# The gain multiplication of a norm moved from VectorE to GpSimd, behind the residual additions

## What is computed

```python
def rms_norm(x, g):
    xf = x.astype(jnp.float32)
    y = xf * lax.rsqrt(jnp.mean(xf * xf, axis=-1, keepdims=True) + RMS_EPS)
    return (y * g.astype(jnp.float32)).astype(x.dtype)

    for layer in range(DEPTH):
        h = h + FFN_RES_SCALE * swiglu(rms_norm(h, ffn1_norm[layer]), ...)
        hn = rms_norm(h, mix_norm[layer])
        ...
        h = h + attention(hn) @ w_o
        h = h + FFN_RES_SCALE * swiglu(rms_norm(h, ffn2_norm[layer]), ...)
        if layer == N_A_LAYERS - 1:
            kv = (rms_norm(h, kv_norm) @ kv_w)
    return rms_norm(h, final_norm)
```

## Time and profile before

| | us |
|---|---|
| three runs | 1777.2, 1777.74, 1778.76 |
| median | 1777.74 |
| profiled execution, first to last instruction (span) | 1775.5 |
| TensorE busy | 1757.9 (99%) |
| VectorE busy | 1184.5 (67%) |
| ScalarE busy | 869.8 (49%) |
| GpSimd busy | 63.4 (4%) |

### The profile page before, as it was taken

How to read it: one execution, slowest core, us unless ns; L and a number is a source line. 1 busy time by engine, 2 the same in 40 slices (tenths; PEclk the granted TensorE clock), 3 DMA queues, 4 the chain that set the end, 5 groups by cost and what they waited for, 6 DMA issues and landing times.

```text
span 1775.5 us, 24760 instructions
## 1 busy us (share of the span) xinstructions
PE 1757.9 (99%) x9869; PEld 1512.3 (85%) x9871; DVE 1184.5 (67%) x1245; ACT 869.8 (49%) x1082; POOL 63.4 (4%) x102
## 2 busy tenths in 40 slices
PE   9999999999999999999999999999999999999998
PEld 7888888888888888888888888888888888788887
DVE  7676576557576575557666666666676666876665
ACT  7545464445555464446343566533354434553343
POOL 1000000000120000000000100000000000210000
PEclk9999999999999999999999999999999999999999
DMA  9526355555556355555655553556556555246652
GB/s 322 179 91 218 119 190 191 190 191 191 187 165 211 133 172 189 189 190 177 201 179 189 194 165 121 177 190 206 178 185 202 179 189 187 98 156 198 196 182 95
DMA packets 215394, 318.03 MB, mean 179 GB/s; under 512 B 5617, under 2 KB 175745, under 8 KB 215314
## 3 DMA queue, kind: packets, MB, share of 16 engines
q1 hardware_dynamic: 210514, 300.96, 50.8%
q0 software_dynamic: 4800, 15.94, 2.8%
HBM read 315.83 MB, written 1.05 MB: 178 GB/s over the span
## 4 chain that ended last, share of the span: by engine, by line
PE 92%; DVE 3%; ACT 3%; issue 1%; POOL 0%; DMA 0%; DVEq 0%; ACTq 0%
PE Y L2094 29%; PE C L1930 22%; PE C L1934 12%; PE C L2033 4%; PE C L1996 3%; PE Y L1907 3%; PE Y L1996 2%; PE C L1998 2%; PE Y L1983 1%; PE Y L1998 1%; ACT w_hi L692 1%; PE C L2052 1%; ACT arena L1010 1%; PE C L2171 1%; PE Y L2306 1%
## 5 line engine op out<-in xcount | busy, mean ns | idle before, releaser
L1232 DVE TENSOR_TENSOR w_lo<-raw,w_hi 128x2048 fp32r<-128x2048 f32 x276 | 631.8, 2290 | 284.6 <-ACT w_hi L692 284.4
L692 ACT ACTIVATE w_hi<-raw 128x2048 fp32r<-128x2048 f32 x282 | 538.5, 1910 | 258.0 <-PE Y L2094 161.4
L1930 PE MATMUL C<-at_hl,w_hi 128*128 128x512 f32 x1424 | 339.1, 390 | 0.0
L1930 PEld LDWEIGHTS C<-at_hl,w_hi 128*128 128x128 f32 x1424 | 264.9, 188 | 53.5
L2094 PE MATMUL Y<-w_hi,hid_h 128*128 128x512 f32 x696 | 216.9, 393 | 0.1
L2094 PE MATMUL Y<-w_lo,hid_h 128*128 128x512 f32 x696 | 215.0, 390 | 0.0
L2094 PE MATMUL Y<-w_hi,hid_l 128*128 128x512 f32 x696 | 214.6, 389 | 0.0
L1934 PEld LDWEIGHTS C<-at_hl,w_lo 128*128 128x128 f32 x1424 | 183.0, 191 | 7.2
L1934 PE MATMUL C<-at_hl,w_lo 128*128 128x256 f32 x1424 | 185.2, 283 | 0.0
L2094 PEld LDWEIGHTS Y<-w_lo,hid_h 128*128 128x128 f32 x696 | 130.7, 188 | 28.1
L2094 PEld LDWEIGHTS Y<-w_hi,hid_l 128*128 128x128 f32 x696 | 130.7, 188 | 27.9
(11 more groups left out here) (337 smaller groups left out, 2276.5 us busy)
## 6 DMA issues: line engine op xcount, KB each, us to landing
raw<-in_ffn_w_in SPq DMA_DIRECT2D x88, 1024.0 KB, 5.1
raw<-in_w_ff SPq DMA_DIRECT2D x64, 1024.0 KB, 5.5
raw<-in_ffn_w_out SPq DMA_DIRECT2D x44, 1024.0 KB, 5.1
raw<-in_w_mem_kv SPq DMA_DIRECT2D x16, 1024.0 KB, 5.8
raw<-in_w_qkv SPq DMA_DIRECT2D x12, 1024.0 KB, 5.3
raw<-in_sb_w_qkv SPq DMA_DIRECT2D x12, 1024.0 KB, 5.2
raw<-in_w_in_ab SPq DMA_DIRECT2D x8, 1024.0 KB, 9.7
raw<-in_w_mem_q SPq DMA_DIRECT2D x8, 1024.0 KB, 5.0
```

The costliest lines, as they stand in the source:

```text
L692: nc.scalar.activation(w_hi[:, n % RING, :], raw[:, n % RAW, :], ACT.Copy).then_inc(hi_split, 1)
L1232: V.tensor_tensor(w_lo[:, n % RING, :], raw[:, n % RAW, :], w_hi[:, n % RING, :].bitcast(f32), ALU.subtract).then_inc(lo_split, 1)
L1930: mm(tiles(C[:, 2 * pair + i, :], 2), wh[:, k, i * P:(i + 1) * P], hl[:, k, :, :], start=k == 0, stop=False)
```

## The change

GpSimd multiplies x by g into `xn`, in two halves per block, as soon as x of the block is ready, and VectorE then multiplies each half in place by r. ScalarE's squares go to a stretch of the arena named `unread`. The list `gained_norms` takes the norms that are `("norm", "ahead")` with an `add` step just before. The diff, whole but for its context:

```diff
@@ build
         relu = [front[:, i * 2 * S:(i + 1) * 2 * S] for i in range(3)]
+        unread = front[:, 0:D]
@@
+        x_gained = sem("x_gained")
@@ behind the counts
+        gained_norms = [at.norm for (s, at), last in zip(before[1:], net) if s == ("norm", "ahead") and last[0] == "add"]
+
+        def x_parts(at):
+
+            return 4 * gained_norms.index(at.norm)
@@ GpSimd, behind the load of the weight row
                         pool.dma_start(gain[:, i % 2, :], gain_rows[i].partition_broadcast(P)).then_inc(gains_in[i % 2], 16)
+                if at.norm in gained_norms and s == ("norm", "ahead"):
+                    pool.wait_ge(gains_in[at.norm % 2], 16 * ((at.norm + 1) // 2))
+                    for b in range(TB):
+                        pool.wait_ge(x_ready, at.x - 1 + b)
+                        for i in range(2):
+                            part = slice(i * 512, (i + 1) * 512)
+                            nc.gpsimd.tensor_tensor(xn[:, b, part], x[:, b, part], gain[:, at.norm % 2, part], ALU.mult).then_inc(x_gained, 1)
@@ ScalarE
-            def guess(src, b, at, shift=0):
+            def guess(src, b, at, shift=0, to=None):
                 j = 2 * at.rms + b
-                nc.scalar.activation(xn[:, b, :], src, ACT.Square, accum_out=stat[:, 0, j:j + 1]).then_inc(squared, 1)
+                nc.scalar.activation(xn[:, b, :] if to is None else to, src, ACT.Square, accum_out=stat[:, 0, j:j + 1]).then_inc(squared, 1)
@@
-            def x_guess(b, at, shift=0):
+            def x_guess(b, at, shift=0, to=None):
                 act.wait_ge(x_ready, at.x - 1 + b)
-                guess(x[:, b, :], b, at, shift)
+                guess(x[:, b, :], b, at, shift, to)
@@ ScalarE, add_ahead
-                x_guess(0, then)
+                x_guess(0, then, 0, unread)
                 hi(then.chunk - 1 + AHEAD)
                 norm_hi("at", then, C, [0])
-                x_guess(1, then)
+                x_guess(1, then, 0, unread)
@@ VectorE
+            def gained_scale(b, at):
+
+                rms(b, at, 0)
+                j = 2 * at.rms + b
+                for i in range(2):
+                    part = xn[:, b, i * 512:(i + 1) * 512]
+                    dve.wait_ge(x_gained, x_parts(at) + 2 * b + i + 1)
+                    V.tensor_scalar(part, part, stat[:, 6, j:j + 1], None, ALU.mult).then_inc(xn_ready, 1)
@@ VectorE, add_ahead
                 add(factor, at, [0])
-                norm_scale("at", then, [0], 0, 2)
+                gained_scale(0, then)
                 add(factor, at, [1])
                 norm_lo("at", then, C, [0])
                 if doubled:
                     lo_part(then.chunk - 1 + AHEAD, 0)
-                    norm_scale("at", then, [1], 0, 2)
+                    gained_scale(1, then)
@@
                 lo_part(then.chunk - 1 + AHEAD, 0)
-                norm_scale("at", then, [1], 0, 2)
+                gained_scale(1, then)
```

## The result

The changed kernel takes 1780.29 us (median of 21 runs, 1780.03 to 1782.34), the kernel before in the same comparison 1777.48 (21 runs). The ratio is 1.0015, with a 95% interval of 1.0010 to 1.0021: 2.8 us slower. I had forecast 1777.5, with a range up to 1780.0.

What follows compares the result with a forecast made beforehand. TensorE bounds the kernel, leaving 1.84 us idle in five passages; terms of -0.10, 0, -0.35, +0.10 and +0.10 sum to -0.25 us, so 1777.74 becomes 1777.5, range 1775.6 to 1780.0.

Steps and rivals of the forecast that it cites:

- What bounds the kernel, and which passages: TensorE busy 1757.9 of 1775.5 us; five passages with 1.84 us idle; two behind an attention can't gain in block 0.
- second half of `w_lo`: Behind block 1's scaling, passages behind an attention: some 0.4 us later with 0.3 us slack, 0.1 lost each.
- VectorE's scaling: Two instructions of 1.41 us become two TENSOR_SCALARs: 0.45 us for the first half, 0.80 for both.
- GpSimd's products: Four per passage, 128x512, 1.04 us each; block 0's in time for VectorE by only 0.1 us.
- (d): GpSimd's product much longer than L606's: decides from about 1.3 us; at twice 1.04, +9 us, 1786.5; chance 0.07.
- The engines exclude each other: VectorE's refining and GpSimd's products wait for each other's whole instruction; block 0's refining ends 0.15 us later.
- Block 1: Stick passage: scaling starts at about 1007.1 instead of 1006.50, just in time; 0.10 gained booked for stick, 0 for `kv_cols`.
- no slack left: Said of block 1 in the stick passage, with GpSimd's products at 1.04 us each.
- The sign that I had named for being wrong: TensorE's turns of block 1 (L2171) waiting over 0.3 us would show the forecast wrong.
- The sum at my own price: Five passages with products at 1.04 us: -0.10 - 0 - 0.35 + 0.10 + 0.10 = -0.25 us.
- The row for "same": Its load goes out at about 1311.3, behind the `kv_cols` products; VectorE stalls 1.0 us, hidden with 1.5 to spare.
- The base: 1777.74 us for the kernel before, the span standing 2.2 us under the median of the runs.

Runs made afterwards that it cites:

- e8: Changed kernel with GpSimd multiplying only the first 512 columns, VectorE scaling the second half as before; 1776.25 us, ratio 0.9994 to the kernel before.
- e2: Changed kernel with GpSimd's product taking one repeated number per row, weight row left out of the five norms; 1777.03 us, ratio 0.9997 to the kernel before.
- e1: Changed kernel with the refining using one tensor input, other factors as numbers per token; 1777.02 us, ratio 0.9998 to the kernel before.
- e7: Changed kernel with the load of the row for "same" moved ahead of the products into kv_cols; 1780.27 us, ratio 1.0013 to the kernel before.
- e11: Changed kernel with GpSimd multiplying each half of x by the other half, weight row left out; 1780.1 us in a single execution.
- e6: Kernel before, with GpSimd also computing x times x into unused memory in the same four pieces; 1780.69 us, ratio 1.0019.
- e9: The first-half-only GpSimd product plus the refining with one tensor input, on the changed kernel; 1776.81 us, ratio 0.9994 to the kernel before.
- e3: Changed kernel without GpSimd products, VectorE scaling x by r alone, weight row left out of the five norms; 1776.10 us, ratio 0.9993 to the kernel before.

## Why the prediction was wrong

- **What bounds the kernel, and which passages.** Right: TensorE, five passages, two of them without a wait for the scaling in block 0. Those two still lost 0.35 each, by block 1's second half of `w_lo`; I had that place and sign, at 0.1.
- **VectorE's scaling.** 0.88 to 0.91 measured for 0.80 booked, 0.49 for 0.45 (e8). Right but for a tenth.
- **GpSimd's products: the step that failed.** I took 1.04 us from L606, a row with a repeated second input, and had named that as the case against it only in rival (d). Measured 1.28. I also had somewhat too high the point from which it decides: I wrote "from about 1.3 us". It lies between the 1.03 of e2 (-0.25 us) and 1.28 (+2.8). With my own sum redone at 1.28, block 0's second product ends 2.7 us after x is ready and holds the refining 0.6 us instead of 0.15 (measured 0.67), and in block 1 both scalings come 0.8 us later than I had worked out (measured: 10.96 us after the first addition for 10.1).
- **The engines exclude each other.** Right in direction and in both orders, and by e1 the condition of the whole loss. By the rule of the Trainium skill ("SBUF — State Buffer", "Who interferes with whom"), a VectorE instruction with two SBUF inputs and a GpSimd instruction that reads SBUF block each other for the whole instruction. The trace agrees: in both blocks the refining ends 0.01 us after GpSimd's product. The Trainium skill's 4497 ns for 2048 columns ("GPSIMD Engine Reference", "Performance versus the Vector engine"), 1.12 us a product by my estimate, is nearer than my 1.04 and still under the 1.28 measured.
- **Block 1.** I found "no slack left" and then booked 0 to 0.1. A path without slack needs its price at the upper bound, not at the taken value. The sign that I had named for being wrong, L2171 of block 1 waiting over 0.3, is there into `kv_cols` (0.40).
- **The sum at my own price.** e2 tests it: -0.37 us of the stretch for my -0.25. By passage it is -0.22, +0.02, +0.03, -0.21 and +0.01, where I had -0.10, +0.10, 0, -0.35 and +0.10. The terms are each off by up to 0.14, and that the total comes near is partly that they cancel.
- **The row for "same".** Loaded at 1314.40, a stall of 1.22 for 1.0 forecast, hidden (e7). Right.
- **Rivals and range.** (d) was the right mechanism with a price between the two that I worked out (1.04 and 2.08). The range ended at 1780.0 because case (d) at its lower edge was left out of it. That the change stayed within 0.2%, as I gave 0.91, is no merit of the sum, which had the other sign.
- **The base.** The 1777.74 was the median of three runs; 21 gave 1777.48. And the span stands 1.9 us under the time of its own execution (1779.7 and 1781.6), not 2.2. Neither bears on the difference.

## What to carry to other kernels

Work moved to GpSimd isn't free for VectorE even where nobody waits for its result: in these runs VectorE instructions with two tensor inputs in SBUF, down to one number per row, stood still for the rest of a GpSimd product. Cut the GpSimd piece so that it ends before the next such instruction (e8), or give that instruction one tensor input and its other factors as numbers per row (e1). And take the price of an operation from a row that has the same operands, not only the same shape.

## What the runs showed of the hardware

- GpSimd's multiplication of 128x512 fp32 takes 1.28 us with two different full inputs (the changed kernel, e11) and 1.03 with a repeated number or the same input twice (e2, e6).
- A TENSOR_SCALAR on one number per row runs at its full pace beside a GpSimd product (0.27 us, e1), one on 512 columns does not (a pair took 1.44 for 0.88, e1).
- In e9's traced execution TensorE, after idling 0.67 and 1.08 us in the swa attention, ran a short while at the lower of its two levels: groups of eight products that take 0.87 us took 1.55, and the granted clock of these 5.2 us is 0.67 (windows: width, busy time by engine, clock, DMA). It lost about 1.7 us by it, against e8; e3's execution had the same at 0.72. The kernel before and e8 idle as long at this place (0.69 and 1.08 us) and keep the clock at 1.00, and e9's and e3's own medians lie 1.9 and 1.3 us under these executions, so it comes and goes between executions of one kernel. What sets it off was not tried.

```profile
1553.02 0.93 PE L2386 MATMUL C<-arena 64*128 64x128 f32 x8 [0.67 <-DVE arena L1611]
...
1555.03 1.55 PE L2406 MATMUL Y<-arena 128*64 128x256 f32 x8 [1.08 <-DVE arena L1638]
```
```profile
1540.00:1554.00 14.00, 13.23 (x96) 9.16 (x94) 13.54 (x40) 7.29 (x24) 5.21 (x6) 1.00 0.20 74
1554.00:1559.20 5.20, 4.17 (x23) 2.80 (x24) 4.06 (x19) 3.99 (x19) 1.34 (x2) 0.67 0.41 139
```
